# RMS norms whose root is multiplied into each projection as VectorE evacuates it, with a head's logarithms and exponentials placed behind its second and third projection group

## The reference, cut to what matters

```python
def rmsnorm(x, g):
    y = x * rsqrt(mean(x * x, axis=-1) + EPS)
    return y * g

u = rmsnorm(h, g_mix);  z = u @ w_in          # GLA, short convolution, window attention, gates
h = h + merged @ w_o
u = rmsnorm(h, g_ffn);  hid = causal_dwconv(u @ w_up)
h = h + (silu(hid[:2816]) * hid[2816:]) @ w_down
x = rmsnorm(h, g_final)                        # end of the first block
h = concat(meta_tokens, x)                     # 16 + 512 positions
u = rmsnorm(h, norm1);  proj = u @ w_in_2      # HGRN2 (8 heads) and Mamba-2 (8 tiles of 2 heads)
h = h + concat(out_a, out_b) @ w_out_2
h = h + conv_glu_ffn(rmsnorm(h, norm2))        # w_up_2, w_down_2
y = rmsnorm(h, final)
```

## Time and profile before

| | |
|---|---|
| three runs | 1867.45, 1869.77, 1870.22 us (median 1869.77) |
| profiled run | 1866.25 us, span 1864.5 us |
| mean granted TensorE clock | 0.985 |
| busy PE / PEld / DVE / ACT | 1784.2 / 1540.9 / 1062.8 / 749.2 us |
| share of the span | 96 / 83 / 57 / 40 % |
| instructions DVE / ACT | 1635 / 1130 |
| weights | 280 loads of 512 KB, 82 GB/s over the span |

### The profile page before, as it was taken

How to read it: one execution, slowest core, us unless ns; L and a number is a source line. 1 busy time by engine, 2 the same in 40 slices (tenths; PEclk the granted TensorE clock), 3 DMA queues, 4 the chain that set the end, 5 groups by cost and what they waited for, 6 DMA issues and landing times.

```text
span 1864.5 us, 27001 instructions
## 1 busy us (share of the span) xinstructions
PE 1784.2 (96%) x11004; PEld 1540.9 (83%) x11004; DVE 1062.8 (57%) x1635; ACT 749.2 (40%) x1130; POOL 8.2 (0%) x10
## 2 busy tenths in 40 slices
PE   5999999999989999999799999989998799999997
PEld 2877777778868888888598989889988699999885
DVE  5455545555466666633556465766787666666323
ACT  4444434332243333322446565544454433333221
POOL 0000000000000000000000000000000000000000
PEclk9999999999999999999899999999999899999999
DMA  4222222222322333333122212122212132332331
GB/s 167 79 79 80 79 90 69 90 80 92 101 68 90 94 99 98 95 94 98 46 80 64 73 58 80 57 69 69 69 61 66 56 91 91 91 93 93 99 101 57
DMA packets 44331, 154.21 MB, mean 83 GB/s; under 512 B 5793, under 2 KB 6049, under 8 KB 44209
## 3 DMA queue, kind: packets, MB, share of 16 engines
q1 hardware_dynamic: 44208, 152.50, 26.6%
HBM read 150.39 MB, written 2.10 MB: 82 GB/s over the span
## 4 chain that ended last, share of the span: by engine, by line
PE 90%; DVE 6%; ACT 2%; issue 1%; SPq 0%; DMA 0%; ACTq 0%; DVEq 0%
PE ps L555 88%; PE ps L559 2%; DVE full L1384 1%; DVE u_lo L1214 1%; ACT arena L848 1%; DVE arena L1217 1%; DVE arena L1224 1%; DVE h_res L1214 0%; ACT r_bc L848 0%; DMA w_raw<-weights 0%; ACT full L848 0%; DVE w_lo L1214 0%; DVE r_bc L1214 0%; DVE h_res L1384 0%; ACT w_hi L848 0%
## 5 line engine op out<-in xcount | busy, mean ns | idle before, releaser
L555 PE MATMUL ps<-u_hi,w_hi 128*128 128x264 f32 (+3 forms) x2376 | 652.4, 328 | 33.1 <-DVE u_lo L1214 30.6
L555 PE MATMUL ps<-u_hi,w_lo 128*128 128x264 f32 (+3 forms) x2376 | 643.3, 324 | 0.0
L555 PE MATMUL ps<-u_lo,w_hi 128*128 128x264 f32 (+3 forms) x2376 | 641.7, 323 | 0.0
L1214 DVE TENSOR_TENSOR w_lo<-w_raw,w_hi 128x1024 fp32r<-128x1024 f32 x280 | 343.0, 1225 | 257.1 <-ACT w_hi L848 241.1
L555 PEld LDWEIGHTS ps<-u_hi,w_hi 128*128 128x128 f32 (+1 forms) x2376 | 396.7, 189 | 88.4 <-issue 34.3
L555 PEld LDWEIGHTS ps<-u_lo,w_hi 128*128 128x128 f32 (+1 forms) x2376 | 396.5, 189 | 36.5 <-issue 1.1
L555 PEld LDWEIGHTS ps<-u_hi,w_lo 128*128 128x128 f32 (+1 forms) x2376 | 397.1, 189 | 35.3 <-issue 1.0
L848 ACT ACTIVATE w_hi<-w_raw 128x1024 fp32r<-128x1024 f32 x280 | 297.0, 1061 | 209.2 <-PE ps L555 174.5
L1224 DVE SCALAR_TENSOR_TENSOR ffn<-ps,par,ffn 128x512 f32<-128x512 f32 (+2 forms) x176 | 132.0, 750 | 163.4 <-ACT ffn L848 160.2
L848 ACT ACTIVATE arena<-ps 128x512 f32<-128x512 f32 (+7 forms) x218 | 97.2, 485 | 239.2 <-PE ps L555 148.3
L848 ACT ACTIVATE ffn<-ps,par 128x512 f32<-128x512 f32 x88 | 64.6, 734 | 296.9 <-PE ps L555 296.9
(11 more groups left out here) (132 smaller groups left out, 1418.2 us busy)
## 6 DMA issues: line engine op xcount, KB each, us to landing
w_raw<-weights SPq DMA_DIRECT2D x280, 512.0 KB, 3.6
h_res<-xT SPq DMA_DIRECT2D x4, 512.0 KB, 5.1
outT<-h_res SPq DMA_DIRECT2D x8, 256.0 KB, 2.1
cst<-consts SPq DMA_DIRECT2D x1, 730.0 KB, 8.5
seg<-consts SPq DMA_DIRECT2D x1, 256.0 KB, 8.7
par<-params SPq DMA_DIRECT2D x1, 243.5 KB, 6.5
msk<-cmask SPq DMA_DIRECT2D x1, 128.0 KB, 8.9
h_res<-metaT SPq DMA_DIRECT2D x1, 64.0 KB, 8.2
```

Of the source, the lines that this page charges most:

```text
L555: return nc.tensor.matmul(out, lhsT, rhs, start=start, stop=stop)
L1214: return V.tensor_tensor(out, a, b, op)
```

## The change: the diff

What it does:
- `raw` takes the place of the second half of a norm: ScalarE writes `u_hi = round(h_res * gain)`, VectorE `u_lo = h_res * gain - u_hi` (one instruction), without the root, behind each group that completes a tile. For the output groups `om` both `raw` and `square` stand one group later.
- TensorE's sum of a norm stands inside the projection that follows (`SUMS_AT`): ahead of `gk 0`, ahead of unit 5 of `up (0,0)`, unit 6 of `hf 0`, and ahead of `up2 (0,1)`. The last norm stays as it was.
- VectorE multiplies every accumulator of a projection by the root as it reads it out (`mul(..., x, r)`); the first such evacuation of each part waits for the root (`ROOT_AT`). ScalarE no longer reads these accumulators: its tanh or convolution tap works on the tile in SBUF, in place or into another tile, after VectorE. The last taps, `silu` and product of an `up` group (`finish_up`) run at the start of VectorE's next group.
- Short convolution: `cc` is multiplied by r squared, the convolution's result by r. Mamba-2 convolution: all four taps by VectorE, taps halved once, the final halving gone. `dt` is multiplied first.
- `norm1`: root and sums of both norms are made from the two sums with EPS squared; `second_start`'s scaling of `h_res` is spread over four steps; the meta tokens' parts are made during `up (2,0)`.
- HGRN2: `prep` is split into `prep_ln` (behind `hq`), `prep_exp` (behind `hi`) and the products (behind `hg`); `f` is finished in `hq`'s group.
- The slots of the second block are exchanged, so that `hf 0` waits for one group of `down` only.
- SP: parameters first, then one load of x, slab 0, the other loads of x, slabs 1 and 2, then the constants.

```diff
 def slot_of(g):
-    return g % SLOTS1 if g < FIRST2 else SLOTS1 + (g - FIRST2) % SLOTS2
+    return g % SLOTS1 if g < FIRST2 else SLOTS1 + (g - FIRST2 + 1) % SLOTS2
...
     for h in range(HG_H):
-        at = [(k, h + 1) for k in names] if h + 1 < HG_H else tail
-        put(names[3], h, ("prep", GLA_H + h))
-        nxt = [(k, h + 2) for k in names] if h + 2 < HG_H else tail if h + 2 == HG_H else (("mc", 1),)
-        for stage, where in zip("abcd", list(at[1:4]) + [nxt[0]]):
-            put(*where, ("head_" + stage, GLA_H + h))
-
+        n = GLA_H + h
+        if h > 1:
+            put("hf", h, ("head_d", n - 2))
+        put("hq", h, ("prep_ln", n))
+        put("hi", h, ("prep_exp", n))
+        if h:
+            put("hq", h, ("head_a", n - 1))
+            put("hi", h, ("head_b", n - 1))
+            put("hg", h, ("head_c", n - 1))
+        put("hg", h, ("prep", n))
...
+SUMS_AT = {GROUP_OF[("gk", 0)]: ("g_mix", 0), GROUP_OF[("up", (0, 0))]: ("g_ffn", 5),
+           GROUP_OF[("hf", 0)]: ("norm1", 6), GROUP_OF[("up2", (0, 1))]: ("norm2", 0)}
+ROOT_AT = {0: "g_mix", GROUP_OF[("up", (0, 0))]: "g_ffn", GROUP_OF[("hf", 0)]: "norm1",
+           GROUP_OF[("up2", (0, 0))]: "norm2"}
...
# ScalarE
+            def raw(which_k):
...
+                residual_ready(act, which, k)
+                c0, c1 = norm_columns(which)
+                f(u_hi[:, k, c0:c1], h_res[:, k, c0:c1], ACT.Identity, scale=gain_of(which, k)).then_inc(u_hi_ok, 1)
...
                 elif kind == "gate":
...
-                    f(mrg[:, KD + n % 2, :], x, ACT.Tanh, scale=0.5).then_inc(free, 1)
+                    gate = mrg[:, KD + MERGE.index(i) % 2, :]
+                    evacuated(act, g)
+                    f(gate, gate, ACT.Tanh, scale=0.5).then_inc(gate_ok, 1)
...
+            def prep_ln(n):
+                exp_ln()
+                act.wait_ge(f_ok, n - GLA_H + 1)
+                f(lf2, f2[n % 2], ACT.Ln).then_inc(sp_ok, 1)
+
+            def prep_exp(n):
+                exp_ln()
+                act.wait_ge(cum_ok, n + 1)
+                act.wait_ge(ready, n)
+                f(e2[:, 0, :], bc2, ACT.Exp)
+                f(e2[:, 1, :], bc2, ACT.Exp, scale=-1.0)
+                f(h_mid, h_mid, ACT.Exp).then_inc(exp_ok, 1)
...
# VectorE
+                dve.wait_ge(u_hi_ok, KD * i + k + 1)
+                V.scalar_tensor_tensor(out=u_lo[:, k, c0:c1], in0=h_res[:, k, c0:c1], scalar=gain_of(which, k),
+                                       in1=u_hi[:, k, c0:c1], op0=ALU.mult, op1=ALU.subtract).then_inc(u_lo_ok, 1)
...
+                if kind == "hq":
+
+                    dve.wait_ge(act_part, PART_NO[GROUP_OF[("hf", i)]])
+                    link(V.tensor_scalar(f2[i % 2], f2[i % 2], lb1[:, i:i + 1], lb[:, i:i + 1], ALU.mult, ALU.add))
+                    V.tensor_scalar(k2, f2[i % 2], -1.0, 1.0, ALU.mult, ALU.add).then_inc(f_ok, 1)
+                product_done(dve, g)
+                if g in ROOT_AT:
+                    dve.wait_ge(rstd_ok, NORMS.index(ROOT_AT[g]) + 1)
...
+                elif kind == "gate":
+                    mul(mrg[:, KD + MERGE.index(i) % 2, :], x, r).then_inc(free, 1)
...
                 elif kind in ("up", "up2"):
-                    j, half = i
...
+                    mul(full[:, g % 2, 0:n], x, r).then_inc(free, 1)
+                    pending[0] = g
...
                 elif kind in ("mb", "mc", "mx"):
...
-                    madd(dst[:, 3:], x[:, 0:T2 - 3], pc("m2conv", 4 * c), dst[:, 3:]).then_inc(free, 1)
+                    mul(out, x, r).then_inc(free, 1)
+                    dve.wait_ge(free, TURN[g] + 1)
+                    link(V.tensor_scalar(dst, out, pc("m2conv", 4 * c + 3), pc("m2convb", c), ALU.mult, ALU.add))
+                    link(madd(dst[:, 1:], out[:, 0:T2 - 1], pc("m2conv", 4 * c + 2), dst[:, 1:]))
+                    link(madd(dst[:, 2:], out[:, 0:T2 - 2], pc("m2conv", 4 * c + 1), dst[:, 2:]))
+                    madd(dst[:, 3:], out[:, 0:T2 - 3], pc("m2conv", 4 * c), dst[:, 3:]).then_inc(S["conv"], 1)
...
             def ssm_gate(t):
-                evacuated(dve, GROUP_OF[("mz", t)])
+                dve.wait_ge(act_part, PART_NO[GROUP_OF[("mz", t)]])
+                link(twice_silu(m_z[t % 2], full[:, t % 2, :], m_z[t % 2]))
```

More of the change, by code:

```diff
@@ L224, in schedule @@
         for k in range(KD):
-            put(kind, at[k], ("square", (which, k)))
+            where = at[min(k + 1, KD - 1)] if kind == "om" else at[k]
+            if which != "final":
+                put(kind, where, ("raw", (which, k)))
+            put(kind, where, ("square", (which, k)))
+        if which == "norm1":
+            put(kind, at[-1], ("bounds", 0))
         put(kind, at[-1], ("norm", which))
-    put("down", KD - 1, ("bounds", 0))
-    put("hf", 0, ("second_start", 0))
-    put("hq", 0, ("second_start", 1))
+    put("up", (2, 0), ("raw_meta", 0))
+    put("hf", 0, ("second_start", 4))
+    for part, where in enumerate((("hq", 0), ("hi", 0), ("hf", 1), ("hq", 1))):
+        put(*where, ("second_start", part))
     put("mc", 1, ("ssm_dt", 0))
@@ L246, in schedule @@
     after[GROUP_OF[("om", (1, 0))]].insert(0, ("ssm_sum", 1))
-    steps = [("square", ("g_mix", k)) for k in range(KD)] + [("norm", "g_mix")]
+    steps = [("raw", ("g_mix", 0)), ("raw", ("g_mix", 1)), ("slab", 0)]
+    steps += [("raw", ("g_mix", k)) for k in range(2, KD)] + [("slab", 1)]
+    steps += [("square", ("g_mix", k)) for k in range(KD)]
     for g in range(NG):
+        if GROUPS[g][:2] == ("gk", 0):
+            steps.append(("norm", "g_mix"))
         steps.append(("group", g))
@@ L1189, in ssm_sum @@
                 f(r, r, ACT.Exp, scale=-0.5).then_inc(S["r"], 1)
-            stages = {"square": square, "norm": norm, "bounds": bounds, "group": group, "prep": prep, "head_a": head_a, "head_b": head_b, "head_c": head_c,
+            stages = {"raw": raw, "raw_meta": raw_meta, "slab": lambda s: split_until(s + 1), "square": square, "norm": norm, "bounds": bounds, "group": group, "prep": prep, "prep_ln": prep_ln, "prep_exp": prep_exp, "head_a": head_a, "head_b": head_b, "head_c": head_c,
                       "head_d": head_d, "swa_v": swa_v, "swa_a": swa_a, "swa_b": swa_b, "ssm_dt": ssm_dt,
@@ L1343, in square, with raw_meta @@
+            def raw_meta(_):
+                dve.wait_ge(meta_hi_ok, 1)
+                for k in range(KD):
+                    last = V.scalar_tensor_tensor(out=u_lo[:, k, 0:META], in0=h_res[:, k, 0:META],
+                                                  scalar=pc("norm1", k), in1=u_hi[:, k, 0:META],
+                                                  op0=ALU.mult, op1=ALU.subtract)
+                last.then_inc(meta_lo_ok, 1)
             def square(which_k):
@@ L1348, in square @@
                 n = c1 - c0
-                if (which, k) == ("g_mix", 0):
-                    V.memset(ones[:, :], 1.0).then_inc(zeroed, 1)
                 if k:
@@ L1393, in low @@
[L1393 to L1396 removed]
                 if which == "final":
+                    dve.wait_ge(rstd_ok, NORMS.index(which) + 1)
                     for k in range(KD):
[L1400 to L1401 removed]
@@ L1654, in ssm_v2 @@
                                        op0=ALU.mult, op1=ALU.subtract).then_inc(tile_lo, 1)
-            stages = {"square": square, "norm": norm, "bounds": bounds, "second_start": second_start, "group": group, "prep": prep, "head_a": head_a, "head_b": head_b,
+            stages = {"raw": raw, "raw_meta": raw_meta, "slab": lambda s: low_until(s + 1), "square": square, "norm": norm, "bounds": bounds, "second_start": second_start, "group": group, "prep": prep, "prep_ln": prep_ln, "head_a": head_a, "head_b": head_b,
                       "head_d": head_d, "swa_a": swa_a, "swa_c": swa_c, "ssm_dt": ssm_dt,
```

407 lines of the change are left out of this document (205 added, 202 removed).

## The result

The changed kernel takes 1874.57 us, the median of 20 runs (1865.57 to 1888.84), against 1868.03 for the kernel before on the same chip (20 runs, 1865.35 to 1870.22): a ratio of 1.0047, 95% interval 1.0024 to 1.007. Forecast were 1826 and a gain. The times of the changed kernel lie in two groups, ten from 1865.6 to 1869.8, level with the kernel before, and ten from 1879.4 to 1888.8, for a reason that wasn't looked into; the median falls into the gap between them, 6 us above the middle of the lower group, and the profiled run belongs to the upper one, 1880.63 us for a span of 1878.8.

The account below looks back on a forecast made before the run. Bound by TensorE's stream and, at four places, the norms' chains. Gains of 55.2 less losses of 13.5 give 41.7 off 1866.25: 1824.5, or 1828 on the median's footing; 1826 us taken, range 1811 to 1847.

Parts of the forecast that it names:

- The four places: Start, `g_ffn`, `norm1`, `norm2`: TensorE's waits and low clock at norms mostly go; gains 14.7, 10.4, 16.3, 13.8, together 55.2 us.
- Window attention: Tanh and a copy wait behind VectorE's multiply, stalling `swa_c` 0.65 in six later steps: -3.9 us, bounds 0 and 10.
- HGRN2: `head_b` stalls 0.5 us in six or seven heads, as tanh waits for VectorE: -3.3 us, bounds 0 and 16.
- In return `prep` is short: HGRN2: with `prep` short, the waits for `hf`'s slot were said to have room; no separate size.
- rivals 2 and 3: Rival 2, and boundaries not closing: late additions, 4 to 6 us waiting plus half clock at three norms; -18, 1843, chance 0.07.
- Mamba-2: More VectorE work and later tanh at `ssm_bc`, `om (0,0)`, last two tiles, `v_lo`: -6.3 us, bounds +3 and -18.
- The cover of `up`, `up2`: Added multiplies in 88 groups cost 0, covered by 2.9 us idle a pair; uncovered 1.4 a pair, 60 us.
- Rival 2: Second block becomes VectorE's: in-order waits in HGRN2 and Mamba-2 plus lower clock, 20 us more, 1846; chance 0.20.
- Rival 1: All VectorE's new work is covered, no stretch above 92% busy: 1813 us; chance 0.15.
- Rival 4: Slower: second block's two slots run out when VectorE is a group late; 43 us and more, 14 in `up2`; 1872, chance 0.04.
- The sign: Gaps above 1 us at every `hq` or `mx`, or before the sums, would make the forecast wrong.
- The rule weighed: Leaving PSUM to ScalarE speaks against the change; rows show no VectorE surcharge (683 against 682 ns), so the sum stands.

Follow-up runs that it names:

- e3: Changed kernel with the next weight slab's low parts (`w_lo`) made behind `prep`'s products on VectorE instead of ahead of them: 1836.73 us, ratio 0.9841.
- e4: Changed kernel with the root of head n-2 taken ahead of `hf`'s tanh on ScalarE instead of behind it: 1840.10 us, ratio 0.9855.
- e9: Changed kernel with ScalarE taking `hf`'s tanh straight from PSUM, the root left out of `hf`: 1845.94 us, ratio 0.9882.
- e10: Changed kernel with tanh's activation table asked for ahead of the waits of `hf`, `hq` and `hg`: 1859.60 us, ratio 0.9957.
- e7: Changed kernel with the edits of e3 and e4 together, plus `prep_ln` placed behind the previous head's `head_a`: 1824.45 us; run once more, 1825.37.
- e8: e7 with `mz 0`'s tanh behind the first tile's exponentials and Mamba-2's first root ahead of `mx 5`'s tanh on ScalarE: 1822.95 us, ratio 0.9759.
- e1: Changed kernel with HGRN2's logarithm, sum and exponentials back behind `hg`, the split of `prep` undone: 1874.06 us, ratio 1.0041.

## Why the prediction was wrong

By its own steps:
- **The four places** hold: 15.2, 10.6, 16.6 and 14.0 against 14.7, 10.4, 16.3 and 13.8. `u_lo`'s 30.6 us of waiting are 0.4, `r_bc`'s 24.3 are the last norm's 2.3. At the start `ga` ends at 16.75 (17), and the guess that the clock rises half-way was right: its first matmuls, from 9.14, start 0.43 us apart, those from 13.3 on 0.23. Group lengths of 6.7, 8.1 and 7.2 were forecast and are 6.4, 7.8 and 7.8.
- **Window attention** -3.9: the stage lost 4.8, with the small gap of half a microsecond at its place.
- **HGRN2** -3.3 with a bound of 16: this step failed. It was measured at -52.3. (The working changes its zero on the way, from `hf`'s end to `hf`'s first matmul, 5.9 earlier; the sum is right all the same.) It began "Take `hf`'s end as 0. Multiply 0.7", which took VectorE to be free when `hf` ends. But in the earlier trace rows `head_d` starts at 1019.04, 6.7 us after `hf`'s end (1004.17 and 8.17), because VectorE comes from `prep` only then. I had only followed ScalarE's chain forward from the read-out, never asked when VectorE reaches it. It reaches it 4.8 us after `hf`'s end, since `w_lo` at the head of `prep` waits for a `w_hi` that stands on ScalarE behind a tanh, which waits for VectorE. So `head_d` on VectorE starts 9.1 us after `hf`'s end in place of 4.6, and `hq` is read out 7 us late. "In return `prep` is short" fell with it. The bound was 2 us a head; the standing alone was 5.8, because the chain of 30.2 us from `hg`'s end was never added up from there and held against TensorE's 24.4. That one chain passes through these places is shown by e3, e4 and e9: three different links, each of which alone gives back 28.6 to 37.8 us.
- **The clock** wasn't in the forecast's price of any loss, only in rivals 2 and 3, though the earlier trace rows showed it at the norms: 3.25 of the 9.0 of a head.
- **A table load** was priced at 1.28 ahead of the logarithm, but not the one ahead of `hq`'s tanh, which here comes behind the wait (e10).
- **Mamba-2** -6.3: measured -13.6, inside its bounds; 5.0 of it is the loop's last head, for in e7 the stage loses 8.6. The chain from `mx 0` gave up 1.1 as priced (3.58 to 4.66 before `ssm_bc`), but behind it the clock is low for 10.24 us where it was 3.42. These are the kernel before and the changed one at this place, then:

```profile
1225.48:1228.90 3.42, 3.00 (x15) 2.61 (x15) 1.84 (x2) 1.72 (x3) 0.00 (x0) 0.50 0.00 0
```

```profile
1245.45:1255.69 10.24, 7.72 (x37) 6.87 (x38) 3.91 (x10) 4.71 (x16) 0.00 (x0) 0.50 0.19 54
```

  Half of the difference, 3.4 us, is time.
- **The cover of `up`, `up2`** at 0 holds: an `up2` pair takes 11.55 us, against 11.53.
- **Rivals.** Rival 2 named this mechanism, in-order waits of a tanh behind its own multiply and of `head_d` for the root with the low clock behind them, but at "1 us or so" in some 60 groups; it was 4 us in head 1 and 6 to 9 in each of heads 2 to 7. Rival 1's "no VectorE stretch is above 92%" overlooks the forecast's own 19.2 of 20.55 us for `om`, 93%. Rival 4 had the size, 1872, though its own terms, 43 and 14 on top of 1826, make 1883, and it had the wrong place: no slot of the second block ran out, TensorE waited for `head_a`'s and `head_b`'s operands.
- **The sign.** "Gaps above 1 us at every `hq`" was named as what would make the forecast wrong: the gap of 2.27 behind `hq` stands in every head from 2 on.
- **The rule weighed.** The read-out in its own duration costs what the rows said, 0.70 to 0.71 for 528 columns. The Trainium skill (Advanced Engine Details and Errata, The Read-Write Bubble) advises PSUM for ScalarE by closeness. The result speaks neither for nor against that: what cost was whose queue the read-out stood in.

With the loop open, e7 takes 1825.4 and the profile's span falls by 41.2 us, where the sum said 41.7. The agreement is partly luck: HGRN2 then loses 0.3 and not 3.3, Mamba-2 8.6 and not 6.3.

One thing stays open here: the 4.7 us behind `mz 0`, which e8 left, has only a read cause.

## What to carry to other kernels

When an evacuation moves from one in-order engine to another, don't ask only what it lasts: list what stands behind the consumer's new wait on its engine (here the last head's root, `w_hi`) and ask whether the engine waited for needs any of it to get there. If it does, follow the chain through both engines until it reaches TensorE again, add it up, and compare it with TensorE's work in the same stretch (30.2 against 24.4 us here). The difference is paid in every round, and busy shares of 50% say nothing of it. Such a loop is opened by moving one statement that waits behind one that doesn't depend on it; try that before giving up a change whose gains are visible elsewhere. And when work is moved away from ahead of a wait (the scan ahead of `w_lo`), ask what it had covered.

## What the runs showed of the hardware that was not expected

- A load of the activation table stood behind the wait of the tanh that needs it at `hq` and `hg` (980.57 and 1002.68 in the changed kernel), but ahead of the wait at `hf` in e1 (1024.11, then 5.58 idle). Asked for by hand, it went ahead at all of them, and a head shrank from 40.9 to 35.8 us.
- Two gaps of 2.25 and 3.53 us, with 9.3 of dense matmuls between them, drew one stretch of the lower clock, behind the second, in heads 2 to 4. A single gap of 1.1 (e4) drew none in heads 2 to 7. Gaps of one size didn't always do the same: 1.4 (e3) drew one in heads 2 and 3 and none in heads 4 to 7, 1.6 (e9) drew one in heads 3 and 6 of seven. What gaps cost is therefore not proportional to them: e4's 1.1 cost 1.1 us, the changed kernel's 5.8 cost 9.0.
- The granted clock that the profile shows can miss the start: the row of the changed kernel's first 16.75 us says 1.00, while the matmuls of 9.14 to 12.96 start 0.43 us apart, against 0.23 later.
